# Two attention pairs to a block in the third stage of a float32 transformer kernel, and its input parts stored by parity

## The reference

```
hn = rms_norm_2(x, ln_g[l])
proj = jnp.einsum('bsd,dc->bsc', hn, w_in[l])
(qa, ka, va, ga, qb, kb, vb, gb, qc, kc, vc, gc, gate_logits) = jnp.split(proj, SPLIT_POINTS, axis=-1)
...
o_a = moba_attention(qa, ka, va, rel_bias[OFF_A:OFF_A + H_A])
o_b = dilated_attention(qb, kb, vb, rel_bias[OFF_B:OFF_B + N_DIL * H_B])
o_c = swa_sink_attention(qc, kc, vc, sinks[l], rel_bias[OFF_C:OFF_C + H_C])
branches = jnp.stack([o_a * silu(ga), o_b * silu(gb), o_c * silu(gc)], axis=2)
br = jnp.einsum('bsiw,iwd->bsid', branches, w_branch[l])
merged = jnp.sum(sigmoid(gate_logits) * br, axis=2)
x = x + jnp.einsum('bsd,de->bse', merged, w_out[l])
```

## Time and profile before

| | us |
|---|---|
| median of 3 timed runs (lowest, highest) | 986.04 (985.62, 986.70) |
| profiled execution | 985.71 |
| its span, first to last instruction | 983.9 |
| PE busy | 975.5 (99%) |
| PE weight loads busy | 795.5 (81%) |
| VectorE busy | 622.7 (63%) |
| ScalarE busy | 591.6 (60%) |

### The profile page before, as it was taken

The page is one execution under the profiler, slowest core; times in us unless marked ns, Lnnn a source line. Parts: engine busy times, 40 slices in busy tenths (PEclk is TensorE's granted clock), DMA queues, the critical chain, the costliest instruction groups (busy, mean ns, idle before and its releaser), DMA issues.

```text
span 983.9 us, 13106 instructions
## 1 busy us (share of the span) xinstructions
PE 975.5 (99%) x4936; PEld 795.5 (81%) x4936; DVE 622.7 (63%) x771; ACT 591.6 (60%) x924; POOL 17.1 (2%) x30
## 2 busy tenths in 40 slices
PE   8999999999999999999999999999999999999998
PEld 7888788888888877788888888877778877788887
DVE  5777766455556767575555465777666657787644
ACT  7777664454546656465454555776667668857571
POOL 2000000000000000000000000000000000000000
PEclk9999999999999999999999999999999999999999
DMA  8535265656563634357656654665444343436651
GB/s 286 175 134 190 86 223 193 227 181 201 171 213 128 214 129 160 112 184 251 220 192 204 205 184 147 175 211 172 136 149 144 109 150 131 140 119 213 201 182 43
DMA packets 106078, 169.37 MB, mean 172 GB/s; under 512 B 4196, under 2 KB 65590, under 8 KB 106032
## 3 DMA queue, kind: packets, MB, share of 16 engines
q1 hardware_dynamic: 103392, 161.23, 50.3%
q0 software_dynamic: 2304, 7.40, 2.3%
q10 hardware_dynamic: 336, 0.10, 0.0%
HBM read 167.56 MB, written 1.16 MB: 171 GB/s over the span
## 4 chain that ended last, share of the span: by engine, by line
PE 95%; DVE 2%; ACT 1%; DMA 1%; issue 1%; SPq 0%; DVEq 0%; ACTq 0%
PE acc L510 14%; PE acc L512 13%; PE acc L511 13%; PE acc L568 12%; PE pair_ps L512 7%; PE pair_ps L510 7%; PE pair_ps L511 7%; PE acc L826 3%; PE acc L627 3%; PE turn_ps L707 2%; PE acc L734 2%; PE turn_ps L586 1%; PE pair_ps L688 1%; PE pair_ps L692 1%; PE acc L662 1%; PE turn_ps L510 1%
## 5 line engine op out<-in xcount | busy, mean ns | idle before, releaser
L1797 DVE TENSOR_TENSOR w_lo<-w_raw,w_hi 128x2048 fp32r<-128x2048 f32 (+3 forms) x154 | 343.1, 2230 | 135.7 <-ACT w_hi L1145 135.3
L1145 ACT ACTIVATE w_hi<-w_raw 128x2048 fp32r<-128x2048 f32 (+3 forms) x154 | 286.4, 1863 | 82.1 <-PE acc L512 31.2
L510 PE MATMUL acc<-w_hi,uT_hi 128*128 128x512 f32 (+3 forms) x552 | 218.8, 396 | 1.0 <-DVE w_lo L2255 1.0
L512 PE MATMUL acc<-w_hi,uT_lo 128*128 128x512 f32 (+3 forms) x552 | 212.0, 384 | 0.0
L511 PE MATMUL acc<-w_lo,uT_hi 128*128 128x512 f32 (+3 forms) x552 | 211.6, 383 | 0.0
L510 PE MATMUL pair_ps<-w_hi,uT_hi 128*128 128x512 f32 x320 | 126.5, 395 | 0.0
L512 PE MATMUL pair_ps<-w_hi,uT_lo 128*128 128x512 f32 x320 | 124.8, 390 | 0.0
L511 PE MATMUL pair_ps<-w_lo,uT_hi 128*128 128x512 f32 x320 | 124.6, 389 | 0.0
L510 PEld LDWEIGHTS acc<-w_hi,uT_hi 128*128 128x128 f32 x552 | 104.4, 189 | 24.3 <-issue 5.1
L512 PEld LDWEIGHTS acc<-w_hi,uT_lo 128*128 128x128 f32 x552 | 104.3, 189 | 20.5
L511 PEld LDWEIGHTS acc<-w_lo,uT_hi 128*128 128x128 f32 x552 | 104.5, 189 | 17.5
(11 more groups left out here) (266 smaller groups left out, 1268.0 us busy)
## 6 DMA issues: line engine op xcount, KB each, us to landing
w_raw<-in_w_in SPq DMA_DIRECT2D x46, 1024.0 KB
w_raw<-in_w_gate SPq DMA_DIRECT2D x44, 512.0 KB
w_raw<-in_w_up SPq DMA_DIRECT2D x44, 512.0 KB
w_raw<-in_w_down SPq DMA_DIRECT2D x22, 1024.0 KB
w_raw<-in_w_out SPq DMA_DIRECT2D x12, 1024.0 KB
w_raw<-in_w_qkv SPq DMA_DIRECT2D x16, 512.0 KB
w_raw<-in_w_branch SPq DMA_DIRECT2D x6, 1024.0 KB
w_raw<-in_w_qkv SPq DMA_DIRECT2D x4, 1024.0 KB
```

Of the source, the lines that this page charges most:

```text
L510: mm(o, xh, wh[:, k, :], start=first and k == 0, stop=False)
L512: done = mm(o, xl, wh[:, k, :], start=False, stop=last and k == len(kts) - 1)
L1145: activation(w_hi[:, slot, 0:width], w_raw[:, slot, 0:width], ACT.Copy).then_inc(hi_done, 1)
L1797: v.tensor_tensor(w_lo[:, slot, 0:width], w_raw[:, slot, 0:width], w_hi[:, slot, 0:width].bitcast(f32), ALU.subtract).then_inc(lo_done, 1)
```

## The change

Four things change, nearly all in the third stage. First, the two input parts `uT_hi` and `uT_lo` are copied once, during the first group, into `oT_hi` and `oT_lo` with the even tokens ahead of the odd ones (`parted`, `in_turn`; four copies on ScalarE, four on VectorE), and groups 1 and 2 project from there. Second, in all five groups logits of pairs 0 and 1 (then 2 and 3) are made in one block, and so are their values; odd pairs have `turn_ps` for their logits and `pair_ps` for their probabilities, and two pairs' results leave `acc[3]` in one copy and turn in one go. The probabilities of a pair are turned alone, some of them in the middle of a unit (`middle`) rather than at its end (`end`). Third, the gates' group gets an order of its own: turns at the end of unit 0, logits in the middle of units 1 and 3. Fourth, in the band mixer two of VectorE's `slot_step` move behind copies of probabilities.

The diff, cut to its core:

```diff
@@ -181,16 +181,20 @@
         def branch_banks(i, half):
             return acc[2:4] if (i, half) != (0, 0) else acc[0:2]
 
+        groups = ("last", "classes")
+
         def logit_tile(kind, t):
 
-            return turn_ps if kind in ("sb", "band") and t % 2 else pair_ps
+            return turn_ps if kind != "mla" and t % 2 else pair_ps
 
         def prob_tile(kind, t):
 
-            return pair_ps if (kind, t) == ("band", 5) else turn_ps
+            return pair_ps if (kind in groups and t % 2) or (kind, t) == ("band", 5) else turn_ps
 
         def out_bank(kind, t):
 
...
+        def in_turn(x, i):
+
+            return x[:, 2 * i:2 * i + 2, :].rearrange("p k (i c) -> p k c i", c=TB)
+
+        def parted(x, i):
+
+            return x[:, 2 * i:2 * i + 2, :].rearrange("p k (c i) -> p k c i", c=TB)
 
         def prob_width(kind):
             return 256 if kind == "classes" else 384
...
@@ -506,7 +515,7 @@
                 for k, kt in enumerate(kts):
                     if n.fresh is not None and blk == 0 and kt % 2 == 0:
                         pe.wait_ge(turned_lo, n.fresh + kt // 2 + 1)
-                    xh, xl = columns(x_hi, kt, blk), columns(x_lo, kt, blk)
+                    xh, xl = x_hi[:, kt, tokens(blk)], x_lo[:, kt, tokens(blk)]
                     mm(o, xh, wh[:, k, :], start=first and k == 0, stop=False)
                     mm(o, xh, wl[:, k, :], start=False, stop=False)
                     done = mm(o, xl, wh[:, k, :], start=False, stop=last and k == len(kts) - 1)
...
             def logits(kind, t, pair0, turn0):
-                pe.wait_ge(qkT_read, turn0 + (t + 1))
-                if kind in copied_ahead:
-                    if t % 2 == 0:
-                        since(pe, logit_read, pair0 + t - 1)
-                    if t in copied_ahead[kind]:
-                        pe.wait_ge(prT_act, pair0 + copied_ahead[kind][t])
-                        pe.wait_ge(prT_dve, pair0 + copied_ahead[kind][t])
+                if kind in groups:
+                    if t < 2:
+                        pe.wait_ge(qkT_read, turn0 + (2, 4)[t])
+                    if t == 2:
+                        pe.wait_ge(prT_act, pair0 + 2)
+                        pe.wait_ge(prT_dve, pair0 + 2)
                 else:
-                    since(pe, logit_read, pair0 + t)
+                    pe.wait_ge(qkT_read, turn0 + (t + 1))
...
+            def turn_outputs(half, pair0, outs):
+
+                pe.wait_ge(out_copied, pair0 + 2 * (half + 1) - 16)
+                pe.wait_ge(out_read, pair0 + 2 * half)
+                for t in range(2):
+                    for blk in range(TB):
+                        done = transpose(acc[2][:, S * t + P * blk:S * t + P * blk + P], outs[half][:, t, P * blk:P * blk + P],
+                                         ident[:, :])
+                done.then_inc(out_turned, 2)
+
+            def two_logits(kind, t, pair0, turn0):
+                for i in range(2):
+                    logits(kind, t + i, pair0, turn0)
+
+            def two_values(kind, t, pair0):
+                for i in range(2):
+                    values(kind, t + i, pair0)
...
+            def project(widths, middle, end, classes=False):
+
+                if classes:
+                    pe.wait_ge(parted_hi, KT // 2)
+                    pe.wait_ge(parted_lo, KT // 2)
+                x_hi, x_lo = (oT_hi, oT_lo) if classes else (uT_hi, uT_lo)
...
+                            if blk == 1:
+                                middle(s)
+                        chunk_unit(x_hi, x_lo, range(k0, k0 + 4), width, k0 == 0, k0 == 4, between)
+                        end(s)
...
+            def project_and_attend(kind, copied, following, qk=None, classes=False):
+
+
+
+                pair0, turn0 = n.pair, n.turn - (0 if qk else 2)
+
+                def middle(s):
+                    if s == 0:
+                        if qk:
+                            first_turns(qk)
+                        for t in range(2, 4):
+                            turn_tokens(t, qk_banks[t])
+                    if s == 2:
+                        turn_probs(kind, 1, pair0)
+                    if s == 4:
+                        turn_probs(kind, 3, pair0)
+
+                def end(s):
+                    if s == 0:
+                        two_logits(kind, 0, pair0, turn0)
+                        if not qk:
+                            turn_outputs(1, pair0 - 4, head_outs)
+                    if s == 1:
+                        turn_probs(kind, 0, pair0)
+                    if s == 2:
+                        two_logits(kind, 2, pair0, turn0)
+                        pe.wait_ge(acc_read, copied)
+                        two_values(kind, 0, pair0)
+                    if s == 3:
+                        turn_probs(kind, 2, pair0)
+                    if s == 4:
+                        two_values(kind, 2, pair0)
+                        turn_outputs(0, pair0, head_outs)
+                    if s == 5:
+                        first_turns(following)
+
+                project((512, 512, 512), middle, end, classes)
+                n.pair = pair0 + 4
...
+            def gates_and_attend(kind, qk, copied, closing):
+
+                pair0, turn0 = n.pair, n.turn
+
+                def middle(s):
+                    if s == 1:
+                        two_logits(kind, 0, pair0, turn0)
+                        turn_outputs(1, pair0 - 4, head_outs)
+                    if s == 2:
+                        turn_probs(kind, 0, pair0)
+                    if s == 3:
+                        two_logits(kind, 2, pair0, turn0)
+                        pe.wait_ge(acc_read, copied)
+                        two_values(kind, 0, pair0)
+                    if s == 4:
+                        turn_probs(kind, 2, pair0)
+                    if s == 5:
+                        two_values(kind, 2, pair0)
+                        closing()
+
+                def end(s):
+                    if s == 0:
+                        pe.wait_ge(qk_ready, qk)
+                        pe.wait_ge(keys_spread, 1)
+                        for t in range(4):
+                            turn_tokens(t, qk_banks[t])
+                    if s == 2:
+                        turn_probs(kind, 1, pair0)
+                    if s == 4:
+                        turn_probs(kind, 3, pair0)
+                        turn_outputs(0, pair0, window_outs)
+                    if s == 5:
+                        turn_outputs(1, pair0, window_outs)
+
+                project((512, 512, 512), middle, end)
                 n.pair = pair0 + 4
...
+                        if 2 <= s:
+                            activation(parted(oT_hi, s - 2), in_turn(uT_hi, s - 2).bitcast(f32), ACT.Copy).then_inc(parted_hi, 1)
                         s += 1
...
+
+                slot_step()
+                exponentiate(kind, 2, pair0, head0)
+
+                def fourth():
+                    exponentiate(kind, 3, pair0, head0)
+                    copy_outputs(kind, 0, pair0, head_outs)
+                    copy_probs(2, pair0, kind)
+                later = chunks[1](fourth)
+
+                slot_step()
+                later()
+                copy_probs(3, pair0, kind)
+
+                copy_outputs(kind, 1, pair0, head_outs)
+                slot_step()
+                chunks[2]()
...
@@ -2019,8 +2206,8 @@
                 norm(0)
                 slot_step()
                 norm(1)
-                slot_step()
                 probs(0)
+                slot_step()
                 tops(2)
                 tops(3)
                 norm(2)
@@ -2064,25 +2251,101 @@
                         after_unit[s]()
                     if s in done:
                         done[s]()
-
-            def project_and_attend(units, kind, head0=0, bias_of=None, done={}, prefetch=(UNIT,) * 6, after_unit={}, late=(), closing={}, last=True):
-                for s in range(6):
...
+                maxima(kind, 0, pair0, head0, bias_of)
+                maxima(kind, 1, pair0, head0, bias_of)
+                if head0:
+                    token_outputs(1, pair0 - 4, head0 - 8)
+
+                slot_step()
+                copy_probs(0, pair0, kind)
+                sums()
+
+                copy_probs(1, pair0, kind)
+                slot_step()
+                maxima(kind, 2, pair0, head0, bias_of)
+                maxima(kind, 3, pair0, head0, bias_of)
+
+                slot_step()
+                norms_of(0)()
+                copy_probs(2, pair0, kind)
+
+                copy_probs(3, pair0, kind)
+                sums()
+                slot_step()
+                token_outputs(0, pair0, head0)
+                norms_of(1)()
+
+                slot_step()
+                keep_sums(head0)
...
+                slot_step()
+                full()
+                maxima(kind, 0, pair0, head0, bias_of)
+                maxima(kind, 1, pair0, head0, bias_of)
```

(30 more changed lines are left out.)

346 lines of the change are left out of this document (204 added, 142 removed).

## The result

The changed kernel takes 978.05 us (median of 6 runs, 977.79 to 979.39) against 985.90 for the kernel before in the same session (6 runs): a ratio of 0.9923, 95% interval 0.9910 to 0.9935. The gain is 7.85 us where 7.1 was forecast. The profiled execution took 978.15 us, with a span of 976.4 (983.9 before).

What follows compares the result with a forecast made beforehand. PE, busy 975.5 of 983.9 us, was taken to bound the kernel. Terms 1.7 + 5.2 + 1.1 + 0.7 - 1.3 - 0.3 = 7.1 us off 985.71 gave 978.6, as median 978.9; range 976.2 to 981.9.

Steps and rivals of the forecast that it cites:

- term 1: Groups 1 and 2: reading parts side by side saves 5.8 ns on each of 288 matmuls, 1.7 us.
- term 2: All five groups: logits and values of two pairs in common blocks save 5.2 us, from 3.6 to 6.2.
- Term 3: End of the third stage: PE's waits of 0.6 and 0.5 us go, 1.1 us back, from 0 to 1.1.
- Term 4: Band mixer: two VectorE splits moved behind copies of probabilities save 0.3 and 0.4 us, together 0.7.
- term 5: New PE waits: 1.3 us for split weights in the gates' group, 0.3 allowed in group 3 and for the gates' second unit.
- the first group of the stage: Third stage's first group: the added copies lie beside unbroken stream and cost 0, at most 2.8 us without that cover.
- The sign that the prediction named: Groups 1 and 2: distance of stream matmuls should be 0.228 us and no longer 0.234.
- the small part of term 5: Group 3's 256-column chunk waiting for ScalarE's copies, and the gates' second unit for a split: 0.3 us, from 0 to 1.1.
- signs of being wrong: Several prT waits in groups 0 to 2, unchanged group distances, or ScalarE's rounding waiting for DMA between 645 and 868 us.
- The upper end of the range: 981.9 us: the stride free, and the two waits at the third stage's end back.
- copies before the values come late: Groups 0 to 2: ScalarE's rounding delays the fourth pair's probabilities, 1.6 us lost in each, 983.7 us; chance 0.09.
- slower: Groups 0 to 2: that rounding also waits for its weights to land, 8.4 us lost, 987.3 us; chance 0.03.

Runs made afterwards that it cites:

- e1: The changed kernel without the copied parts, groups 1 and 2 reading every second token of `uT` again; 979.62 us, ratio 0.9925.
- e2: The changed kernel with VectorE's old order in the band mixer; 979.40 us, ratio 0.9930.
- e3: The changed kernel with one VectorE weight split moved ahead of the maxima of pairs three and four in the gates' group; 977.23 us, ratio 0.9901.
- e4: The changed kernel with VectorE's copy of the last pair's probabilities ahead of the second split in the band mixer; 977.75 us, ratio 0.9905.
- e6: The changed kernel with the second pair's values 12 stream matmuls later, in their own block, in groups 0 to 2; 979.10 us, ratio 0.9933.
- e11: The changed kernel with e3, e4, e7 and e8 together, and two pairs' probabilities turned in one place in groups 0 to 2; 975.80 us, ratio 0.9897.
- e5: The changed kernel with groups 1 and 2 taking every fourth token from two slices of the copied parts, for timing only; 981.74 us, ratio 0.9956.
- e9: The changed kernel itself, run again beside two later versions; 977.66 us, ratio 0.9920.
- e7: e4 plus ScalarE's copy of the third chunk's first token block ahead of rounding the next weights, in the third stage's first group; 976.48 us, ratio 0.9900.
- e8: e4 plus the POOL queue's 1 KB store of row scales put off until group 0's first unit is done; 976.57 us, ratio 0.9902.

## Why the prediction was right, and where it was off

| term | forecast | measured |
|---|---|---|
| 1, contiguous parts | 1.7 | 1.33 (e1) |
| 2, two pairs side by side | 5.2 | about 6.8 (what the other terms leave of the groups' 7.56) |
| 3, two waits at the end | 1.1 | taken as 1.1 (both rows gone) |
| 4, band mixer | 0.7 | 0.63 (e2) |
| 5, new waits | -1.3, -0.3 | -1.49 (e3), -0.2 |
| the first group of the stage | 0 | -0.25 in the pair shown; beside the shortest (238.4) 0 to -1.1 with this order, -4.2 in e4 |

The groups' 7.56 us and the band mixer's 0.63, less 0.25 in the first group (238.89 in place of 238.64 from the end of the band mixer to group 0) and less 0.40 at the start, make the 7.5 between the two spans. That the total came so near the forecast is in part luck: term 2 gave 1.6 more, and term 1, the first group and the start took back 1.0.

Term 1 was right in its mechanism. The size was 5.8 ns for each matmul, and the undoing gives 4.6. The sign that the prediction named was there: the steps within the stream of group 1 (those under 0.28 us) average 0.234 us before, 0.229 in the changed kernel and 0.233 in e1. Of the 0.77 us, 132 matmuls at 4.6 ns make 0.61; what made the other 0.16 in the old order stays open.

Term 2 was mis-sized on the side of the "classes". Group 1 gained 46.92 - 44.82 - 0.68 = 1.42 us beside the stride (1.25 forecast); group 2 gained 44.26 - 42.30 - 0.65 = 1.31 where 0.72 was forecast. I had priced a pair in a common block at what a single one took before, 0.65 and 0.58. In the changed kernel two pairs' logits take 755.53 - 754.34 = 1.19 and their values 756.55 - 755.53 = 1.02, so 0.60 and 0.51 a pair, which makes 0.5 over four pairs; and e6 shows that a pair's values taken out of their block cost 0.4 us. For groups 0 and 3 and the gates' group the table's 6.8 is a remainder, which no run takes apart.

```profile
754.34 0.50 PE L704 MATMUL pair_ps<-qkT 64*128 64x128 f32 x4
...
755.53 1.09 PE L751 MATMUL acc<-prT,qkv 128*64 128x128 f32 x16
756.55 0.50 PE L519 MATMUL acc<-w_hi,oT_hi 128*128 128x512 f32 x1
```

Term 3 has no run of its own: the two waits are absent from all the traces after, and their 1.1 us is taken from the earlier trace rows. Term 4 and the large part of term 5 were right in place, cause and size; both came from writing down what stands behind a waiting instruction on VectorE. For the small part of term 5 there is one step of 0.32 us in place of 0.12, where the second half of the 256-column chunk in group 3 begins (806.17 to 806.49); that it is a wait for ScalarE's copies no run shows.

None of the signs of being wrong appeared: no wait for prT stands in groups 0 to 2, the distances moved, and ScalarE does not wait for DMA between 645 and 868 us. The upper end of the range does not come out of its own terms (980.6 and 1.1 make 981.7, not 981.9); nothing hangs on it.

The rival "copies before the values come late" did not happen in groups 0 to 2 (e11 made it happen). The "slower" rival had the right mechanism, a rounding that waits for its weights with work for PE queued behind it, at the wrong place: I had read the wait of 3.07 us at 638 as harmless where it stood, because PE was not late there before. It had no cover left, as PE's step of 0.31 shows. The step that failed is the cost of nothing for what lies in the first group. Most of that cost is the earlier PE, since e1 has no copies and waits too; but the added copies, which the prediction put at 0, have a part. PE begins `acc[0]` so in e1, without copies, and in e3, with them:

```profile
643.94 0.47 PE L524 MATMUL acc<-w_hi,uT_hi 128*128 128x512 f32 x1 [0.54 <-ACT qkv L1343]
```

```profile
644.20 0.47 PE L519 MATMUL acc<-w_hi,uT_hi 128*128 128x512 f32 x1 [0.76 <-ACT qkv L1339]
```

PE's matmul before it starts at 643.01 and 643.05, and ScalarE's first rounding at 638.10 and 637.99. In e3 the second rounding even starts earlier (641.02, against 641.31 in e1), but then a copied part (642.84) takes 0.55 us right ahead of the copy that empties the bank, which starts at 643.39 in place of 643.13.

How much is lost follows when the first rounding gets its weights, counted from the end of the band mixer. With the changed kernel's order at this place that is 229.0 to 229.2 us in e5, e6 and e9, which lose nothing; 230.0 in the changed kernel and e2, which lose 0.4 to 0.5; 230.5 in e3, which loses 1.1; and 231.7 in e4, which loses 4.2, the lower clock included. It differs between executions of one kernel too: the changed kernel has 230.0 in the first trace and 229.1 in e9.

## What to carry to other kernels

When work ahead of a stage gets shorter, look in that stage for instructions that end at a fixed time (a DMA that lands), and for what is queued behind them on the same engine: a wait without cost today has its cover counted in the microseconds that you are about to save. Where an engine prepares both the next weights and empties the banks of the last product, put the emptying first (e7 and its four close times). And price a tile in a common block by its distance in a common block, not by that of one that stands alone.

## What the runs showed of the hardware

- From 625 to 630 us, while weights were being loaded and a store of 1 KB of row scales was under way, the DMA engines were 87% busy and moved 43 GB/s (e7); with the store put off they were 71% busy and moved 227 GB/s (e8).
- After 2.37 us in which PE waited, its granted clock was 0.50 to 0.51 (1.2 GHz) from 644.75 to 648 us, and matmuls came 0.43 us apart in place of 0.23 (e4). After the wait of 1.2 us in the gates' group of the changed kernel matmuls went on 0.23 us apart behind a first step of 0.34.
- Weight loads of 128 x 128 float32 took 188 ns contiguous, 195 with every second element and 310 with every fourth (there from two slices); at 310 the matmuls still came 0.235 us apart inside a run, and the first distance behind the turns of group 1 rose from 0.31 (changed kernel) to 0.43 (e5).
